# A hybrid MLA/S5 decoder step on one core: the head's input loads reordered, the first weight block cut one tile earlier, the state-space angles moved in between the tiles

## What is computed

```python
for i in range(DEPTH):                       # DEPTH = 2
    hp = _rmsnorm(xp, norm_mix[i]); hs = _rmsnorm(xs, norm_mix[i])
    if i % N_MIXERS == 0:
        w = (mla_w_in[j], mla_q_norm[j], mla_kv_norm[j], mla_w_q_up[j], mla_w_kv_up[j], mla_w_o[j])
        op, ckv_p, kpe_p = _mla_prompt(hp, *w)           # starts with proj = h @ w_in
        osm, ckv_s, kpe_s = _mla_sample(hs, cache_ckv[j], cache_kpe[j], page_table, *w)
    else:
        op, re_p, im_p = _s5(hp, None, None, *w)
        osm, re_s, im_s = _s5(hs, state_ssm_re[j], state_ssm_im[j], *w)
    xp = xp + op; xs = xs + osm
    xp = xp + _mlp(_rmsnorm(xp, norm_mlp[i]), mlp_w1[i], mlp_w2[i])
    xs = xs + _mlp(_rmsnorm(xs, norm_mlp[i]), mlp_w1[i], mlp_w2[i])
```

## Time and profile before

| what | value |
|---|---|
| median of 3 runs | 1558.95 (1557.3 to 1559.12) |
| the profiled execution's own time | 1558.09 |
| its span | 1556.4 |
| granted TensorE clock, mean | 0.979 |
| PE busy | 1483.8 (95%) |
| DVE / ACT / POOL busy | 739.6 (48%) / 591.9 (38%) / 334.8 (22%) |

### The profile page before, as it was taken

The page is one execution under the profiler, slowest core; times in us unless marked ns, Lnnn a source line. Parts: engine busy times, 40 slices in busy tenths (PEclk is TensorE's granted clock), DMA queues, the critical chain, the costliest instruction groups (busy, mean ns, idle before and its releaser), DMA issues.

```text
span 1556.4 us, 31850 instructions
## 1 busy us (share of the span) xinstructions
PE 1483.8 (95%) x11449; PEld 1414.6 (91%) x11449; DVE 739.6 (48%) x1205; ACT 591.9 (38%) x1076; POOL 334.8 (22%) x390
## 2 busy tenths in 40 slices
PE   5999999799998999999999998799999999999997
PEld 5977787689887999999999998699999999999997
DVE  3875556455553544422344555954444433344332
ACT  6354555556543333211233333343333311233222
POOL 0258778434300022100122231000012100122000
PEclk9999999799998999999999998999999999999998
DMA  7114334333323222222222646313222322222221
GB/s 182 27 50 129 109 97 124 113 104 93 104 70 109 82 82 81 81 81 83 80 81 85 224 132 185 125 53 89 83 68 83 93 81 81 80 82 81 82 68 61
DMA packets 248928, 147.75 MB, mean 95 GB/s; under 512 B 46159, under 2 KB 243254, under 8 KB 247830
## 3 DMA queue, kind: packets, MB, share of 16 engines
q1 hardware_dynamic: 242506, 138.94, 31.0%
q0 software_dynamic: 5664, 6.67, 1.6%
q10 hardware_dynamic: 684, 1.18, 0.2%
HBM read 128.48 MB, written 18.26 MB: 94 GB/s over the span
## 4 chain that ended last, share of the span: by engine, by line
PE 89%; DVE 4%; ACT 2%; issue 2%; SPq 1%; DMA 1%; ACTq 0%; DVEq 0%
PE bank L891 64%; PE bank L811 6%; PE bank L1216 3%; PE bank L1020 3%; PE bank L1181 3%; PE bank L958 2%; PE bank L979 1%; PE bank L1009 1%; PE bank L1028 1%; DVE tmpa L2508 1%; DVE arena L2535 1%; DVE sq L2508 1%; DVE rstd L1967 0%; PE bank L1045 0%; SPq L411 0%
## 5 line engine op out<-in xcount | busy, mean ns | idle before, releaser
L891 PE MATMUL bank<-arena_parts,wR 128*128 128x288 f32 x4224 | 566.1, 296 | 4.2 <-ACT arena_parts L1542 3.7
L891 PEld LDWEIGHTS bank<-arena_parts,wR 128*128 128x128 f32 x4224 | 563.0, 188 | 5.2 <-issue 4.9
L891 PE MATMUL bank<-side_parts,wR 128*128 128x288 f32 x3360 | 447.4, 295 | 1.1 <-DVE tmpa L2580 1.1
L891 PEld LDWEIGHTS bank<-side_parts,wR 128*128 128x128 f32 x3360 | 445.5, 188 | 1.5 <-issue 1.3
L1988 DVE TENSOR_TENSOR wR<-wraw,wR 128x1024 fp32r<-128x1024 f32 x159 | 232.8, 1464 | 239.6 <-ACT wR L1526 238.2
L776 POOL TENSOR_TENSOR arena_parts<-sq,arena_parts 128x576 f32 x64 | 91.5, 1430 | 730.8 <-ACT arena_parts L1798 730.8
L1526 ACT ACTIVATE wR<-wraw 128x1024 fp32r<-128x1024 f32 x159 | 167.0, 1050 | 202.0 <-PE bank L891 187.5
L1463 ACT ACTIVATE arena<-bank 128x256 f32<-128x256 f32 (+8 forms) x211 | 87.2, 436 | 96.8 <-PE bank L979 45.8
L1795 ACT ACTIVATE tmpa<-bank 128x576 f32<-128x576 f32 x64 | 41.7, 651 | 195.5 <-PE bank L891 195.5
L2431 DVE TENSOR_TENSOR sq<-tmpa 128x576 f32<-128x576 f32 x64 | 48.5, 759 | 127.2 <-ACT tmpa L1795 127.2
L2359 DVE TENSOR_TENSOR kpR<-bank,rstd 128x576 f32<-128x576 f32 x32 | 24.2, 757 | 127.9 <-PE bank L891 127.9
(11 more groups left out here) (309 smaller groups left out, 1543.1 us busy)
## 6 DMA issues: line engine op xcount, KB each, us to landing
wraw<-in_mlp_w SPq DMA_DIRECT2D x128, 512.0 KB, 4.0
side<-in_cache_ckv SPq DMA_DIRECT2D x128, 128.0 KB, 2.2
wraw<-in_ssm_w_glu SPq DMA_DIRECT2D x16, 512.0 KB, 3.9
s_state_to_out<-side SPq DMA_DIRECT2D x16, 256.0 KB, 2.6
s_in_to_state<-yblk SPq DMA_DIRECT2D x8, 512.0 KB, 3.4
s_in_to_out<-side SPq DMA_DIRECT2D x64, 64.0 KB
wraw<-in_mla_w_o SPq DMA_DIRECT2D x8, 512.0 KB, 5.6
side<-s_in_to_state SPq DMA_DIRECT2D x2, 2048.0 KB, 11.0
```

What stands on the lines that cost most here:

```text
L891: return pe.matmul(bank[:, a, 0:HALF], wR[:, s, wp, k, :], tokens(k, xp)[:, a * HALF:(a + 1) * HALF], start=(first and j == 0), stop=(last ...
```

## The change

In SP's list the prompt tokens come in three column parts of 2, 2 and 4 tiles instead of two of 4, and the first weight block stands behind the first part; the first part counts on the sampled tokens' semaphore. In PE's list two tiles are turned ahead instead of three. In ACT's list the three loads of the poles come last; the first Exp stands behind tile 1 together with the first weight block's cut (it was behind tile 2), and the other Exp and the two Sin stand behind tile 3. In DVE's list the eight instructions on the angles stand behind tile 1, ahead of the first weight block's rest.

```diff
+            def tokens_in(c0, c1, signal):
+                cols = slice(c0 * P, c1 * P)
                 sp.dma_start(xnat[:, 0:BLK, cols], ...)\
-                    .then_inc(x_in[half], 16)
-            for m in range(4):
+                    .then_inc(signal, 16)
+            def input_weights(m):
                 sp.dma_start(wraw[:, m, :, :], col(w_in, 0, IN_COL[m])).then_inc(w_loaded[m], 16)
+            tokens_in(0, 2, smp_in)
+            input_weights(0)
+            tokens_in(2, 4, x_in[0])
+            tokens_in(4, 8, x_in[1])
+            for m in range(1, 4):
+                input_weights(m)
...
-            pe.wait_ge(smp_in, 16)
+            pe.wait_ge(smp_in, 32)
...
             def turn_tile(k):
-                pe.wait_ge(x_in[k // 4], 16)
                 if k >= 2:
+                    pe.wait_ge(x_in[k // 4], 16)
                     pe.wait_ge(tile_free, k - 1)
...
             def first_block():
-                for k in range(3):
+                for k in range(2):
                     turn_tile(k)
...
-                    if k + 3 < KT:
-                        turn_tile(k + 3)
+                    if k + 2 < KT:
+                        turn_tile(k + 2)
...
-            act.dma_start(nat[0:GP, 2, 0:2], I["ssm_log_dt"][0]...).then_inc(a_in, 16)
-            act.dma_start(nat[0:GP, 0, :], flat(I["ssm_a_re"])).then_inc(a_in, 16)
-            act.dma_start(nat[0:GP, 1, :], flat(I["ssm_a_im"])).then_inc(a_in, 16)
             act.dma_start(ident[:, :], I["c_ident"]).then_inc(head_in, 16)
...
-            act.wait_ge(a_in, 16 * 3)
-            act.activation(nat[0:GP, 2, 2:4], nat[0:GP, 2, 0:2], ACT.Exp).then_inc(aprep, 1)
-            act.wait_ge(dprep, 1)
-            act.activation(nat[0:GP, 25, :], nat[0:GP, 23, :], ACT.Exp)
-            act.activation(nat[0:GP, 26, :], nat[0:GP, 24, :], ACT.Sin)
-            act.activation(nat[0:GP, 27, :], nat[0:GP, 24, :], ACT.Sin, scale=0.5).then_inc(aprep, 1)
+            act.dma_start(nat[0:GP, 2, 0:2], I["ssm_log_dt"][0]...).then_inc(a_in, 16)
+            act.dma_start(nat[0:GP, 0, :], flat(I["ssm_a_re"])).then_inc(a_in, 16)
+            act.dma_start(nat[0:GP, 1, :], flat(I["ssm_a_im"])).then_inc(a_in, 16)
...
                 cut_scaled(k, V_MIX)
-                if k == 2:
+                if k == 1:
+                    act.wait_ge(a_in, 16 * 3)
+                    act.activation(nat[0:GP, 2, 2:4], nat[0:GP, 2, 0:2], ACT.Exp).then_inc(aprep, 1)
                     cut_block(0)
+                if k == 3:
+                    act.wait_ge(dprep, 1)
+                    act.activation(nat[0:GP, 25, :], nat[0:GP, 23, :], ACT.Exp)
+                    act.activation(nat[0:GP, 26, :], nat[0:GP, 24, :], ACT.Sin)
+                    act.activation(nat[0:GP, 27, :], nat[0:GP, 24, :], ACT.Sin, scale=0.5).then_inc(aprep, 1)
...
-            dve.wait_ge(aprep, 1)
...
-            dve.tensor_scalar(th, th, lim, -lim, ALU.min, ALU.max).then_inc(dprep, 1)
+            def angles():
+                dve.wait_ge(aprep, 1)
+                ...
+                dve.tensor_scalar(th, th, lim, -lim, ALU.min, ALU.max).then_inc(dprep, 1)
             clear_acc()

             dve.wait_ge(head_sb, 1)
             for k in range(KT):
                 rest_scaled(R_A, k, V_MIX)
-                if k == 2:
+                if k == 1:
+                    angles()
                     cut_rest(0)
```

More of the change, by code:

```diff
@@ L442, in _ @@
             sp.dma_start(xnat[0:NS, BLK, :], I["x_sample"].rearrange("b q n -> (b q) n")).then_inc(smp_in, 16)
-            for half in range(2):
-                cols = slice(half * (D // 2), (half + 1) * (D // 2))
+            def tokens_in(c0, c1, signal):
+                cols = slice(c0 * P, c1 * P)
                 sp.dma_start(xnat[:, 0:BLK, cols], I["x_prompt"][0].rearrange("(t p) n -> p t n", p=P)[:, :, cols])\
-                    .then_inc(x_in[half], 16)
-            for m in range(4):
+                    .then_inc(signal, 16)
+            def input_weights(m):
                 sp.dma_start(wraw[:, m, :, :], col(w_in, 0, IN_COL[m])).then_inc(w_loaded[m], 16)
+            tokens_in(0, 2, smp_in)
[4 more added lines that the diff above has]
+                input_weights(m)
             for a, part in enumerate(("re", "im")):
@@ L1475, in _ @@
             flat = lambda a: a[0].rearrange("g p -> (g p)").rearrange("(q n) -> q n", n=P)
-            act.dma_start(nat[0:GP, 2, 0:2], I["ssm_log_dt"][0].rearrange("(q a) -> q a", a=2)).then_inc(a_in, 16)
-            act.dma_start(nat[0:GP, 0, :], flat(I["ssm_a_re"])).then_inc(a_in, 16)
-            act.dma_start(nat[0:GP, 1, :], flat(I["ssm_a_im"])).then_inc(a_in, 16)
             act.dma_start(ident[:, :], I["c_ident"]).then_inc(head_in, 16)
@@ L1487, in _ @@
                 at += k
-            act.wait_ge(a_in, 16 * 3)
-            act.activation(nat[0:GP, 2, 2:4], nat[0:GP, 2, 0:2], ACT.Exp).then_inc(aprep, 1)
-            act.wait_ge(dprep, 1)
-            act.activation(nat[0:GP, 25, :], nat[0:GP, 23, :], ACT.Exp)
-            act.activation(nat[0:GP, 26, :], nat[0:GP, 24, :], ACT.Sin)
-            act.activation(nat[0:GP, 27, :], nat[0:GP, 24, :], ACT.Sin, scale=0.5).then_inc(aprep, 1)
+            act.dma_start(nat[0:GP, 2, 0:2], I["ssm_log_dt"][0].rearrange("(q a) -> q a", a=2)).then_inc(a_in, 16)
+            act.dma_start(nat[0:GP, 0, :], flat(I["ssm_a_re"])).then_inc(a_in, 16)
+            act.dma_start(nat[0:GP, 1, :], flat(I["ssm_a_im"])).then_inc(a_in, 16)
             act.wait_ge(head_done, 1)
@@ L2006, in _ @@
             pr, pi = (lambda k: nt(3 + k)), (lambda k: nt(12 + k))
-            dve.wait_ge(aprep, 1)
[L2008 to L2021, removed]
-                settle()
-            lim = 3.1415925
-            dve.tensor_scalar(th, th, lim, -lim, ALU.min, ALU.max).then_inc(dprep, 1)
+            def angles():
+                dve.wait_ge(aprep, 1)
+                dt_ = nat[0:GP, 2, 2:4].unsqueeze(2).to_broadcast([GP, 2, ST])
+                two = lambda a: a.rearrange("p (a n) -> p a n", a=2)
+                own(tt(two(dtr), two(ar), dt_, ALU.mult))
+                own(tt(two(th), two(ai), dt_, ALU.mult))
+                settle()
+                magic = 1.5 * 2.0 ** 23
+                own(dve.tensor_scalar(t1, th, 1.0 / (2 * math.pi), magic, ALU.mult, ALU.add))
+                settle()
+                own(dve.tensor_scalar(t1, t1, -magic, None, ALU.add))
+                settle()
+                c1, c2 = 6.28125, 2029.0 / 2 ** 20
+                for part in (c1, c2, 2 * math.pi - c1 - c2):
+                    own(dve.scalar_tensor_tensor(out=th, in0=t1, scalar=-part, in1=th, op0=ALU.mult, op1=ALU.add))
+                    settle()
+                lim = 3.1415925
+                dve.tensor_scalar(th, th, lim, -lim, ALU.min, ALU.max).then_inc(dprep, 1)
             clear_acc()
```

## The result

| | before | changed |
|---|---|---|
| median, 22 runs each, beside each other | 1557.85 (1554.92 to 1560.57) | 1560.97 (1559.03 to 1564.18) |
| ratio | | 1.0018, 95% interval 1.0012 to 1.0024 |
| the profiled execution's own time | 1558.09 | 1559.03 |
| span, mean granted clock | 1556.4, 0.979 | 1557.4, 0.981 |

A forecast was written before the change was run, and what follows sets the result against it. PE bounds the kernel (95% busy), so the head only shifts its start: -1.55 + 0.15 + 1.9 + 2.0 = +2.5, giving 1560.6 profiled and a median of 1561.5; range 1558.6 to 1565.0.

The forecast's parts named there:

- Earlier start: ACT's queue in the head: with the poles' loads behind, PE's first transpose starts 1.55 earlier, at about 9.14.
- SP's order: SP's loads of token parts and first weight block in another order: 0, since SP waits for none.
- Gate one tile earlier: First weight block cut behind two tiles instead of three: 0, since ACT's work in the head is a sum.
- First Exp: The small Exp in ACT's list ahead of the first weight block's cut: +0.15, with no table load.
- Angles: Eight instructions in DVE's list delay the first weight block's rest, for which PE waits: +1.9.
- Exp, load, Sin: Exp, table load and two Sin behind tile 3 on ACT, with nothing to cover them: +2.02.
- The 1.41: ACT's row behind the gate: tile 3 copied 1.41 after tile 2, read from 21.55 to 22.96 before.
- twenty matmuls at the lower clock: Clock's long form, first block: the 16 + 4 last matmuls take 2.9 more, total up to +6.5.
- most of it is hidden: Rival: faster landing, cheaper angles and Exp, half the pause behind tile 3 hidden; sum -0.65, 1558.3; chance 0.10.
- The longer table load: Rival: ACT also stands still for a drain behind the table load, 1.28 more, +3.8, 1562.8; chance 0.03.
- Absorbed: Rival: slack behind the head takes up the delay, no change, 1559; chance 0.06.
- The clock rival: Rival: PE's clock falls to 1.2 GHz in the new 2.0 pause; about +1.5, total +4.0, 1563.0; chance 0.27.

The follow-up runs named there:

- e1: The changed kernel with DVE making the first weight block's rest ahead of the angles; ratio to the kernel before 1.0008.
- e4: As e3, but ACT cuts the first weight block ahead of everything, DVE makes its rest before the angles, Exp and Sin behind tile 1; 1553.49, ratio to before 0.9970.
- e7: The changed kernel with the gate (first Exp, first block's cut, angles, rest) behind three tiles, three turned ahead; ratio to before 1.0017.
- e8: The changed kernel with the two Sin replaced by scaled copies of the same size, so no table load; ratio to before 1.0006.
- e5: The kernel before with only ACT's three loads for the poles issued last; ratio to before 1.0022.
- e6: The kernel before with only SP's order of loads changed; ratio to before 1.0004.
- e2: The changed kernel with Exp, table load and two Sin behind the first weight block's cut instead of behind tile 3; ratio to before 1.0004.
- e3: The changed kernel with first Exp ahead of tile 0, angles ahead of DVE's first rest, Exp and Sin at the gate as in e2; ratio to before 0.9994.

## Why the prediction was right

The forecast was 1561.5 and +2.5, the runs gave 1560.97 and +2.8. That the time itself was met within 0.5 is in part luck: the forecast stood on a median of three runs that is 1.1 above that of the 22, and its shift was a little too small. The mechanism is what the rows bear out. Term by term, in the order of the prediction:

- *Earlier start, -1.55.* Measured -1.37 (10.69 to 9.32) in the first pair. The load was issued 1.77 earlier (4.27, worked out was 4.49), but took 5.01 to land and not 4.60. Over all profiles the start scatters: 10.69 to 11.11 with the poles' loads in front (4 profiles), 9.26 to 10.16 behind them in the changed kernel and e1 to e4, e7, e8 (9 profiles). With the poles' loads behind and SP's old order (e5) it is 8.95. The size was right to 0.2; the bounds (-2.85 to -0.95) were wide enough.
- *SP's order, 0.* Held, within the scatter (e6 and its repeat), with up to some 0.4 later landing left open. It gave no gain of its own; e4 makes use of it.
- *Gate one tile earlier, 0.* Held to 0.6 (e7), and what is left speaks against the change. A part of it is a wait behind the pause: PE's turn of the tile after next ends at 28.51, and ACT copies it 1.41 behind the one before it (27.14 to 28.55), where it took 1.30 in e7.
- *First Exp, +0.15.* Measured 0.10 (14.31 to 14.41).
- *Angles, +1.9.* Measured 1.82 (15.45 to 17.27) in the changed kernel and 1.78 by e1.
- *Exp, load, Sin, +2.02.* Measured 2.01 in place. Taken away it was worth 1.4 (e2) to 1.8 (e3), because it had itself covered some waiting for PE.
- *Left out.* Tile 3 came 1.77 behind tile 2, not 1.41, and the last four tiles took 5.31 and not 5.20. These 0.47 are what the second cut (31.17, forecast 30.70) was off. The 1.41 was read from one profile, in which the clock had just risen. The second profile of the kernel before has 1.82 in the same place, and both profiles of SP's order have 1.81, so the larger part of the 0.47 isn't a cost of the change but of that early rise in the profile that the forecast started from.

In the first pair the sum is -1.37 + 0.10 + 1.82 + 2.01 + 0.36 + 0.11 = +3.0, which is the second cut's shift, and PE's blocks carry it on. In the second pair it is -1.36 + 0.09 + 1.82 + 2.01 = +2.6 without the last two, and the second cut moved by 2.48. So the second cut moved by 3.01 and by 2.48, where the forecast had 2.54, and the interval of the runs, 1.9 to 3.7, holds all three.

Two of the prediction's side sums don't come out of its rows. Both bounds together, of the landing and of the angles, give a shift of +0.5 to +3.5, where it wrote +1.2 to +3.3. And twenty matmuls at the lower clock are 2.65 more (0.53 for each four, by 1.31 and 0.78), not 2.9. Neither bears on the forecast.

The rivals: "most of it is hidden" fell, ACT's rows show each term in full. The longer table load fell (e8). "Absorbed" fell: +3.03 stands at 35.12 and +3.17 at 957. The clock rival is real, and it was seen in one profile of four: the changed kernel's two show no fall behind the 2.06 pause, one of e1's two does, and there it cost about 0.5 up to the second cut and 1.3 more in the 16 matmuls (3.62 against 2.29). Four profiles of the pause are too few to say whether its chance of 0.27 was fair, and since 2.05 was followed by a fall and 2.06 twice was not, the length that the prediction gave (about 1.5 to 2) doesn't decide it.

## What to carry to other kernels

Work that is hidden under a start-up transfer is free only while some wait covers it. Before moving it so that the transfer can be shortened, look for the next wait of the same engine (here ACT's 3.5 us at the gate, DVE's idle time before its first tile) and put it into that; e3 does, and its rows keep the gain that the change gave away. And if a wait is long because one operand is prepared late, prepare that operand first, in the time when nothing else can run: moving the gate by one tile (e7) made no difference in time that could be told, removing it (e4) gave 0.3%.

For effects of 2 or 3 us in 1558, time many runs and read the cause from a row: the second cut moved by 3.0 in a pair of profiles whose total times differed by 0.9, and by 2.5 in a pair whose total times differed by 6.3. A row scatters too (28.16 and 29.15 in two profiles of the kernel before), so a term that rests on a single profile, as the 1.41 did, wants a second one.

## What the runs showed of the hardware

- The landing of the same small loads behind the same traffic scatters: PE's first transpose, which waits for them, by 0.42 in two profiles of one kernel (10.69 and 11.11) and by 0.90 over seven kernels with one order of loads (9.26 to 10.16).
- A pause of about 2 us on PE is followed by a fall to 1.2 GHz in one profile and not in another of the same kernel (behind 2.05 but not behind 1.75 in e1's two; 2.06 twice in the changed kernel, without a fall).
- The clock's first rise comes at different times in one kernel: in the two profiles of the kernel before the first short turn starts 2.9 and 4.7 behind the first matmuls of the weight block (22.27 and 24.52, behind 19.36 and 19.80), and the stretch from the gate's tile to the second cut is 0.56 longer with the later rise.
- A table load costs 1.4 in a row of small activations, all told (2.01 against 0.60 in e8).
